# Two transformer blocks on one core: alternating row halves of small products, one matmul per norm sum, pairs of output tiles, and the order of the first chunks

## The reference

```python
# block 1
z = rms_norm(x) @ w_in                    # glu, q, k, v, gates
a = silu(rms_norm(conv31(a_val * sigmoid(a_gate))))
y_a = a @ w_conv_out
y_b = dilated_attention(q, k, v) @ w_attn_out      # 16 heads of 64
x = x + (g_a * y_a + g_b * y_b) @ w_out
u = conv3(rms_norm(x) @ w_up);  x = x + (silu(u_g) * u_v) @ w_down
# block 2
z = rmsnorm(x) @ w_in_2      # c_q, c_kv, k_rope, g_q, g_k, g_v, g_lr, og, gates
y_a = mla(rmsnorm(c_q), rmsnorm(c_kv), rope) @ mla_w_o      # 8 heads
y_b = gla(g_q, g_k, g_v, decays) @ gla_w_o   # gated linear attention, chunks of 64
x = x + (sigmoid(gate_a) * y_a + sigmoid(gate_b) * y_b) @ w_out_2
x = x + (silu(rmsnorm(x) @ w_gate) * (rmsnorm(x) @ w_up_2)) @ w_down_2
return rmsnorm(x) * final_norm
```

## Time and profile before

| | us |
|---|---|
| median of 3 runs (lowest to highest) | 859.64 (858.44 to 860.53) |
| the profiled execution's own time | 860.56 |
| its span, first to last instruction | 858.7 |
| PE busy | 840.1 (98%) |
| DVE busy | 649.0 (76%) |
| ACT busy | 555.3 (65%) |
| POOL busy | 233.5 (27%) |

### The profile page before, as it was taken

The page is one execution under the profiler, slowest core; times in us unless marked ns, Lnnn a source line. Parts: engine busy times, 40 slices in busy tenths (PEclk is TensorE's granted clock), DMA queues, the critical chain, the costliest instruction groups (busy, mean ns, idle before and its releaser), DMA issues.

```text
span 858.7 us, 16588 instructions
## 1 busy us (share of the span) xinstructions
PE 840.1 (98%) x6016; PEld 779.7 (91%) x6016; DVE 649.0 (76%) x1163; ACT 555.3 (65%) x1015; POOL 233.5 (27%) x248
## 2 busy tenths in 40 slices
PE   8999999999999999999999999999999999999996
PEld 8998998999999999999889888999988888888885
DVE  7998989996988997777776577847588866566552
ACT  8778999896656776666456765476556656565441
POOL 0387843343211343332111100020022232222111
PEclk9999999999999999999999999999999999999999
DMA  7666654445565475565656444435346466655631
GB/s 264 217 200 183 183 155 155 153 135 171 180 187 169 136 213 193 175 194 177 222 177 177 133 156 129 132 124 167 115 148 189 165 202 182 187 192 160 233 125 50
DMA packets 43024, 146.12 MB, mean 170 GB/s; under 512 B 4912, under 2 KB 7232, under 8 KB 42944
## 3 DMA queue, kind: packets, MB, share of 16 engines
q1 hardware_dynamic: 42336, 144.52, 53.9%
q10 hardware_dynamic: 608, 0.55, 0.2%
HBM read 144.00 MB, written 1.05 MB: 169 GB/s over the span
## 4 chain that ended last, share of the span: by engine, by line
PE 86%; DVE 6%; ACT 3%; issue 2%; DMA 1%; POOL 0%; DVEq 0%; SPq 0%; ACTq 0%
PE px L535 21%; PE px L539 15%; PE px L541 15%; PE px L540 15%; PE px L536 11%; DVE wlo L1398 2%; PE px L545 1%; PE px L547 1%; PE px L546 1%; DVE hx L1415 1%; PE px L758 1%; PE px L610 1%; ACT whi L900 1%; PE px L622 1%; DMA raw<-ws 1%
## 5 line engine op out<-in xcount | busy, mean ns | idle before, releaser
L1398 DVE TENSOR_TENSOR wlo<-raw,whi 128x1024 fp32r<-128x1024 f32 x265 | 332.4, 1261 | 30.5 <-ACT whi L900 30.3
L900 ACT ACTIVATE whi<-raw 128x1024 fp32r<-128x1024 f32 x265 | 277.8, 1052 | 58.9 <-PE px L536 28.9
L539 PE MATMUL px<-hx,whi 128*128 128x256 f32 x1024 | 296.2, 289 | 3.8 <-DVE wlo L1398 1.5
L541 PE MATMUL px<-hx,wlo 128*128 128x256 f32 x1024 | 289.6, 283 | 0.0
L540 PE MATMUL px<-hx,whi 128*128 128x256 f32 x1024 | 289.6, 283 | 0.0
L539 PEld LDWEIGHTS px<-hx,whi 128*128 128x128 f32 x1024 | 196.0, 191 | 7.5 <-issue 2.7
L540 PEld LDWEIGHTS px<-hx,whi 128*128 128x128 f32 x1024 | 196.2, 192 | 0.4
L541 PEld LDWEIGHTS px<-hx,wlo 128*128 128x128 f32 x1024 | 196.1, 191 | 0.0
L2003 POOL TENSOR_TENSOR CA<-CA,ct 128x256 f32<-128x256 f32 x90 | 89.8, 998 | 98.9 <-DVE wlo L1398 76.8
L535 PE MATMUL px<-fx,whi 128*128 128x512 f32 x330 | 115.6, 393 | 0.0
L535 PE MATMUL px<-hx,whi 128*128 128x512 f32 x320 | 113.4, 399 | 0.9 <-DVE wlo L1398 0.6
(11 more groups left out here) (314 smaller groups left out, 1334.9 us busy)
## 6 DMA issues: line engine op xcount, KB each, us to landing
raw<-ws SPq DMA_DIRECT2D x265, 512.0 KB, 3.6
tb<-tabs SPq DMA_DIRECT2D x16, 128.0 KB, 3.5
X<-xs SPq DMA_DIRECT2D x4, 256.0 KB, 3.8
raw<-ws SPq DMA_DIRECT2D x4, 256.0 KB, 5.0
out<-X SPq DMA_DIRECT2D x4, 256.0 KB, 2.4
vc<-vecs SPq DMA_DIRECT2D x1, 315.5 KB, 6.5
msk<-lmask ACTq DMA_DIRECT2D x1, 256.0 KB, 2.8
ug<-pos ACTq DMA_DIRECT2D x1, 128.0 KB, 3.6
```

Of the source, the lines that this page charges most:

```text
L539: e.matmul(b[:, 0:S], H, xh, start=first, stop=False)
L541: m = e.matmul(b[:, 0:S], L, xh, start=False, stop=end)
L900: e.activation(whi[:, n % NSL, :], raw[:, n % NRAW, :], ACT.Copy).then_inc(s_hi, 1)
L1398: e.tensor_tensor(wlo[:, n % NSL, :], raw[:, n % NRAW, :], whi[:, n % NSL, :], ALU.subtract).then_inc(s_lo, 1)
```

## The change

- `ALL_ADDED`: for n2, mix, cq, ckv and ffn the last square is added on DVE too, and `sums` is one matmul. DVE adds the last tile after `low_gained`, and both tiles of cq and the one of ckv between weight remainders; POOL's add for cq is gone.
- `products`, `chunk_sums` and `linear_out` go through the halves of the partitions alternately. In `linear_out` all full-height products come first.
- `turn_probs` stands before `pair_values` in block 1.
- ACT's queue issues half (0,0) of the first chunk; half (0,1) is rounded after the seventh tile; chunk 7's rounding stands after `first_high(5)`.
- ACT multiplies the final gain into `X` right after each square of the last norm, and DVE scales two tiles at a time with `tensor_tensor`; POOL and ACT have no part behind `rms`.

```diff
-                if n > 2:
-                    e.wait_ge(s_add, FROM["add"][inst] + n - 2)
-                else:
-                    e.wait_ge(s_sq, FROM["sq"][inst] + 1)
+                if inst in ALL_ADDED:
+                    e.wait_ge(s_add, FROM["add"][inst] + n - 1)
+                    e.matmul(b[:, 0:S], ones[:, :], sqa[:, half, :], start=True, stop=True, skip_group_check=True).then_inc(
+                        s_sum, 1)
+                    return
+                e.wait_ge(s_add, FROM["add"][inst] + n - 2)
...
+                if 0 <= n - 3 < NH:
+                    turn_probs(0, n - 3, sP)
                 if n >= 5 and n % 2:
                     pair_values(0, (n - 5) // 2, VT, sT)
-                if 0 <= n - 3 < NH:
-                    turn_probs(0, n - 3, sP)
...
-                for par in range(2):
-                    o = 64 * par
-                    for i in range(4):
-                        p_, t = i // 2, i % 2
+                for i in range(4):
+                    p_, t = i // 2, i % 2
+                    for par in range(2):
+                        o = 64 * par
...
-                for ci in range(3):
+                for p_, ci in ((0, 0), (0, 1), (1, 0), (1, 1), (0, 2), (1, 2)):
...
-                    for p_ in range(2):
-                        for ci in range(1, 4):
-                            m = e.matmul(b[:, p_ * S + ci * 64:p_ * S + ci * 64 + 64], gs[o:o + 64, ci - 1, p_, :],
+                for p_ in range(2):
+                    for ci in range(1, 4):
+                        for par in range(2):
+                            o = 64 * par
+                            m = e.matmul(bs[par][:, p_ * S + ci * 64:p_ * S + ci * 64 + 64], gs[o:o + 64, ci - 1, p_, :],
...
+            e.dma_start(raw[:, 0, half(0)], ws[0][:, half(0)]).then_inc(s_half[0], 16)
             e.preload_act_table_set(LOG)
...
                 if i == 3:
                     half_high(0, 0)
-            half_high(0, 1)
+                elif i == 6:
+                    half_high(0, 1)
...
-            for i in (5, 6, 7):
+            first_high(5)
+            highs(7)
+            for i in (6, 7):
                 first_high(i)
             early_gate(2)
-            highs(7)
...
                 square(inst, i, X[:, i, :])
+                if not g:
+                    e.activation(X[:, i, :], X[:, i, :], ACT.Copy, scale=vec("final_norm_2", i)).then_inc(s_og, 1)
...
+            def add_square(inst, i):
+                e.wait_ge(s_sq, FROM["sq"][inst] + i + 1)
+                if i > 1:
+                    e.wait_ge(s_add, FROM["add"][inst] + i - 1)
+                acc = sqa[:, NORMS[inst][1], :]
+                e.tensor_tensor(acc, acc, sq[:, sq_slot(inst, i), :], ALU.add).then_inc(s_add, 1)
...
+                    add_square(inst, i)
...
             beside(FIRST[3])
+            add_square("cq", 1)
+            add_square("cq", 2)
             beside(("ckv", 1))
+            add_square("ckv", 1)
             beside(("kr", 0))
...
-            for i in (0, 1, 3, 4, 6, 7):
-                e.scalar_tensor_tensor(out=X[:, i, :], in0=X[:, i, :], scalar=vec("final_norm_2", i), in1=rst[:, 1, 0:S],
-                                       op0=ALU.mult, op1=ALU.mult).then_inc(s_ov, 1)
+            R = rst[:, 1:2, 0:S].to_broadcast([P, 2, S])
+            for i in range(0, KD, 2):
+                e.wait_ge(s_og, i + 2)
+                e.tensor_tensor(X[:, i:i + 2, :], X[:, i:i + 2, :], R, ALU.mult).then_inc(s_ov, 1)
...
-            add_square("cq", 1)
...
-            half_load(0, 0)
...
+            for i in range(0, KD, 2):
+                e.wait_ge(s_ov, i // 2 + 1)
+                e.dma_start(outv[:, i:i + 2, :], X[:, i:i + 2, :]).then_inc(s_out, 16)
```

More of the change, by code:

```diff
@@ L210 @@
 SQ_AT = {"cq": 0, "ckv": 2}
+ALL_ADDED = ("n2", "mix", "cq", "ckv", "ffn")
 NT_AT = {"cq": 3, "ckv": 0}
 def norm_counts():
-    steps = {"sq": lambda k, n: 4 if k == "n1" else n, "add": lambda k, n: 3 if k == "n1" else max(n - 2, 0), "sum": lambda k, n: 1, "rms": lambda k, n: 1,
+    steps = {"sq": lambda k, n: 4 if k == "n1" else n, "add": lambda k, n: 3 if k == "n1" else n - 2 + (k in ALL_ADDED), "sum": lambda k, n: 1, "rms": lambda k, n: 1,
              "nt": lambda k, n: n * (k not in ("cs", "fin")), "nhi": lambda k, n: n * (k not in ("cs", "fin")),
@@ L436, in two_blocks @@
         s_cor = sem("s_cor")
-        s_ov, s_og, s_oa = sem("s_ov"), sem("s_og"), sem("s_oa")
+        s_og, s_ov = sem("s_og"), sem("s_ov")
         FROM = norm_counts()
@@ L775, in chunk_sums @@
                     e.wait_ge(*BANK[("gv", 0), t])
-                for ci in range(3):
+                for p_, ci in ((0, 0), (0, 1), (1, 0), (1, 1), (0, 2), (1, 2)):
                     o, t = 64 * (ci % 2), ci // 2
-                    for p_ in range(2):
-                        m = e.matmul(bs[ci][:, p_ * S:p_ * S + S], kd[o:o + 64, t, p_ * P:p_ * P + P],
-                                     gv[o:o + 64, t, p_ * S:p_ * S + S], start=(p_ == 0), stop=True, skip_group_check=True)
-                    m.then_inc(s_cu, 1)
+                    m = e.matmul(bs[ci][:, p_ * S:p_ * S + S], kd[o:o + 64, t, p_ * P:p_ * P + P],
+                                 gv[o:o + 64, t, p_ * S:p_ * S + S], start=(p_ == 0), stop=True, skip_group_check=True)
+                    if p_ == 1:
+                        m.then_inc(s_cu, 1)
             def linear_out():
@@ L789, in linear_out @@
                 for par in range(2):
-                    b, o = bs[par], 64 * par
+                    b = bs[par]
                     for p_ in range(2):
@@ L796, in linear_out @@
                                      start=(p_ == 0 and t == 0), stop=False, skip_group_check=True)
-                    for p_ in range(2):
-                        for ci in range(1, 4):
-                            m = e.matmul(b[:, p_ * S + ci * 64:p_ * S + ci * 64 + 64], gs[o:o + 64, ci - 1, p_, :],
+                for p_ in range(2):
[3 more added lines that the diff above has]
+                            m = e.matmul(bs[par][:, p_ * S + ci * 64:p_ * S + ci * 64 + 64], gs[o:o + 64, ci - 1, p_, :],
                                          qL[o:o + 64, p_, ci * 64:ci * 64 + 64], start=False, stop=True,
                                          skip_group_check=True)
-                    m.then_inc(s_go, 1)
+                            if p_ == 1 and ci == 3:
+                                m.then_inc(s_go, 1)
             def linear_sums():
@@ L1377, in _ @@
             rms("fin", D)
-            for n, i in enumerate((2, 5)):
-                e.wait_ge(s_og, n + 1)
-                e.activation(X[:, i, :], X[:, i, :], ACT.Copy, scale=vec("final_norm_2", i)).then_inc(s_oa, 1)
         @block.vector
@@ L1432, in _ @@
                     half_low(0, 0)
-            half_low(0, 1)
+                elif i == 6:
+                    half_low(0, 1)
             half_low(1, 0)
@@ L2104, in _ @@
             ffn(1)
-            e.wait_ge(s_rms, FROM["rms"]["fin"] + 1)
-            for i in (2, 5):
-                e.tensor_tensor(X[:, i, :], X[:, i, :], rst[:, 1, 0:S], ALU.mult).then_inc(s_og, 1)
         @block.sync
```

## The result

The changed kernel takes 849.63 us, median of 4 runs (847.24 to 850.42). The kernel before took 859.04 beside it (857.42 to 860.53, 4 runs), so the ratio is 0.9886, with a 95% interval from 0.9859 to 0.9914: 9.4 us faster. The forecast was 850.8, with a range from 848.8 to 853.4.

The account below looks back on a forecast made before the run. PE, busy for 98% of the span, was taken to bound the kernel, so time counts only where PE does or waits less. The terms sum to 8.8, and 859.64 less 8.8 gives 850.8, range 848.8 to 853.4.

Parts of the forecast that it names:

- start, up to chunk 2: Kernel start: one issue fewer in SP's queue brings later transfers forward, 0.2 (bounds 0 and 0.48).
- chunk 7: Start: rounding in ACT's idle stretch lets DVE's remainder begin 0.73 sooner and PE's wait goes, 0.5 (bounds 0 and 0.6).
- transposes: Attention: transposes ahead of values save 0.15 for each step followed by scores, 0.5 in sum.
- sums of n2, mix, ffn: One matmul per sum instead of two saves 0.43 each, 1.3 in all (bounds 0 and 1.3).
- cq and ckv: Adds on DVE: PE gains 2.5, but the ACT and DVE chain to products(2) gives 1.4 (0.4 to 2.5).
- products 2 to 6: Alternating halves save 0.47 a call in five calls, 2.35; calls 0 and 1 are swallowed by a wait.
- the end: Final output: DVE's four adds of two tiles end at 854.8 instead of 855.74, 0.9 (0.5 to 1.2).
- (1): Rival: chain between cq and products(2) gives only 0.4, or an ACT-bound stretch swallows the start; 852.0, chance 0.14.
- (3): Rival: alternating halves does nothing, only a head start of four records ever overlaps; 854.8, chance 0.05.
- (4): Rival: each switch between halves in products and linear_out drains the array, 0.20 each, 60 switches; 866.8, chance 0.02 (slower).
- The rule of strict program order: Products: old order had no overlap, so alternating gives 0.9 a call; time near 848.6, chance 0.01.
- (2): Clock rival: one more PE stretch at 0.50 makes 852.5 (chance 0.13), one less 849.1 (chance 0.10).

Follow-up runs that it names:

- start_old: The changed kernel with the four halves of the first two weight chunks loaded, rounded and split in the old order; 848.83, ratio 0.9877.
- chunk7_old: The changed kernel with ACT rounding chunk 7 behind the three roundings of the first tiles again; 850.22, ratio 0.9889.
- values_first: The changed kernel with the values of a pair of heads again ahead of the next head's transposes; 850.82, ratio 0.9888.
- adds_on_pool: The changed kernel, single sums kept, with the three adds of squares for cq and ckv on POOL instead of DVE; 850.96, ratio 0.9910.
- halves_apart: The changed kernel without alternation of the halves in products and in the 64-row part of linear_out; 852.61, ratio 0.9932.
- tail_old: The changed kernel with the output scaled as before, six tiles by DVE, two by POOL and ACT; 850.51, ratio 0.9892.
- chain_first: The changed kernel with DVE's remainders of kr, gq 0 and gq 1 moved behind the gate latent; 848.26, ratio 0.9882.
- two_by_two: The changed kernel with products ordered as two of one half, then two of the other; 847.66, ratio 0.9878.
- chain_and_keys: The changed kernel with DVE's remainders of kr, gq 0 and gq 1 and also ACT's two key copies moved later; 846.12, ratio 0.9857.

## Why the prediction was right, term by term

| step | predicted | measured | by |
|---|---|---|---|
| start, up to chunk 2 | 0.2 | 0 to 0.4, open | start_old |
| chunk 7 | 0.5 | 0.65 | chunk7_old |
| transposes | 0.5 | 0.55 to 0.65 | the table; values_first |
| sums of n2, mix, ffn | 1.3 | 1.3 | the table |
| cq and ckv | 1.4 | 1.55 | the table; adds_on_pool |
| products 2 to 6 | 2.35 | 2.5 | halves_apart |
| `linear_out` | 1.65 | 1.65 | 5.03 to 3.37 |
| the end | 0.9 | 1.26 | tail_old |

**The reading held.** PE's distances set the time nearly everywhere, and where a chain sets it, what PE saves ahead of it is lost (`products(0)` and `(1)`). DVE's stretch without a pause kept the transposes' gain out of sight until 198, but what was gained ahead of it came through less 0.2. That the chain from cq on gives 1.4 and not the 2.5 of PE's own savings was its most uncertain term: `scaled` for cq now starts at 478.12 instead of 481.81, of which 2.3 were already there, so 1.4; PE's waits between 470 and 522 sum to 3.5 after and 3.2 before, although the one for POOL is gone. The chain was not wholly as the prediction named it: between the scan and `products(1)` it holds a weight's transfer beside ACT's and DVE's work. That took 4.7 from issue to landing before and 4.6 after, so it hardly entered here; in chain_first it did. By the Trainium skill (SBUF — State Buffer, "SBUF: two separate sides") a GpSimd op that reads SBUF and a DVE op with two SBUF inputs exclude each other for a whole instruction; adds_on_pool agrees, with 4.12 beside three remainders (3.48 in a row) and 0.72 for the same add without them, and DVE's remainders take no more time for it.

**The sizes that were off.** The end gave 0.36 more than its 0.9, though it had been bounded at 1.2. DVE's part was nearly that (3.49 to 2.50, 1.0); what was missing is the landing of the last pair: the span now ends 2.35 after the last issue instead of 2.58. That holds in every profile with the new end (2.34 to 2.36) and with the old one (2.57 to 2.58); its cause is open. The other misses are at most 0.15 each, the start left aside. Chunk 7: DVE's remainder moved by 0.8, and 0.65 of it came through, where the forecast went by the 0.6 that PE had waited. Products: the forecast took `products(2)`, 1.50 from start to start, for all five, but (3) to (6) took 1.53. The chain of cq gave 1.55 for 1.4. All of them have one sign.

**The rivals.** (1) is refuted: the chain gave 1.55, and chunk 7's part came through. (3) is refuted by halves_apart, 2.9 slower by the medians and 3.4 by the traces. (4) is refuted by the products' 1.11: seven switches in a call cost nothing that shows, for 16 records in two rows of eight at 0.11 would take 0.9 and the change of shape behind them 0.1, which is the measured 1.04 from start to next. The rule of strict program order is refuted by two_by_two: by the Trainium skill (TensorE: Matmul & The Clock Gate, "The mechanism") matmuls stay in program order, and the four-record groups would then have kept most of the old time, which they did not; the record that starts ahead of three earlier ones shows it directly. The measurement decides. The prediction's price for this rule, 0.9 a call, set out from a call of 1.8, while its rows already had 1.50. (2), the clock, was rightly named as a size (1.5 to 1.7) and wrongly tied to the kernel: it is neither gained nor lost with the change, it comes in some executions of either kernel.

**The number.** The terms as measured sum to between 9.5 and 10.0; the lowest times of the two kernels differ by as much (856.89 and 847.24, 9.65). The medians differ by 9.4, and the forecast's 8.8 stands at the lower side by the misses above. Of the 1.2 between the forecast and the measured median, 0.6 is the gain and 0.6 is that the kernel before came out at 859.04 beside it and not at 859.64. The profiled executions differ by 13.3, and that number misleads: 2.1 of it is the feed-forward's record distance and 1.5 the stretch at the lower clock.

## What to carry to other kernels

Where two row halves of the matrix engine work on independent products, issue them in turn, at most two matmuls of one before the other (shown here for float32 products of 64 rows and 64 columns); but count the gain only behind the last wait for another engine's chain. Where such a chain rules, follow it on the engines that make it, and move out of it what PE does not need yet: here weight remainders and key copies, worth another 1.45. A weight's landing can be a link of such a chain. Before a difference of two profiles is divided among parts, profile the same kernel twice.

## What the runs showed of the hardware that was not expected

- **A stretch of 3.41 us at the lower of TensorE's two levels** (granted 0.50, which is 1.2 GHz, against 2.4) stands behind `products(2)` in 6 of 14 profiles of both kernels and their variants, always behind the same wait for `qL` and its small products, and costs 1.50. The same program with the same wait had it in one execution and not in the other. By the Trainium skill (TensorE: Matmul & The Clock Gate, "Part 1: The HAM clock gate") the monitor of activity runs freely and does not restart with a kernel; that fits, but no run here varied the phase by itself.
- **The distance of matmuls in the feed-forward** is 0.1766 from record to record in some executions and 0.1735 in others, constant within one, which makes 2.1 us. The times of the profiled executions, and the lowest times, fit these two effects: the kernel before at 860.56 with both, at 859.26 with the distance alone, and at 856.9 to 857.5 in other executions, without a profile; the change at 847.24 with neither and at 848.95 with the stretch alone; chain_and_keys at 848.39 with the distance and at 845.75 to 846.14 otherwise. The cause of it is open. Both profiles of the kernel before had the longer distance; that it has the shorter one too is not shown by a trace and rests on those lowest times, 1.8 to 2.4 below 859.26.
- **A matmul of the other row half starts ahead of up to three records that stand before it**, for float32 with 64 rows and 64 columns. With four records of one half in front it starts within 0.01 of the first of them (two_by_two); with eight in front it starts within 0.01 of the fifth (the old order, 0.47 after the first).
